# Eight row norms in a two-part transformer kernel: turning unscaled rows and multiplying the root in later

## What is computed

```python
def rms_norm(x, g):
    xf = x.astype(jnp.float32)
    y = xf * lax.rsqrt(jnp.mean(xf * xf, axis=-1, keepdims=True) + NORM_EPS)
    return (y * g.astype(jnp.float32)).astype(x.dtype)

h2 = rms_norm(x, g_ffn[l])
gt = causal_dwconv(h2 @ w_ffn_gate[l], ffn_conv_w[l])       # no convolution in the last two layers
x = x + (jax.nn.silu(gt) * (h2 @ w_ffn_up[l])) @ w_ffn_down[l]
```

## Time and profile before

| | us |
|---|---|
| median of 3 runs | 2024.78 (2019.59 to 2033.89) |
| the profiled execution | 2016.36 |
| its span, first to last instruction | 2014.3 |
| PE busy | 1810.7 (90%) |
| DVE / ACT / POOL busy | 1085.8 / 927.5 / 504.2 |
| weights and inputs read | 299.51 MB, 151 GB/s |

### The profile page before, as it was taken

The page is one execution under the profiler, slowest core; times in us unless marked ns, Lnnn a source line. Parts: engine busy times, 40 slices in busy tenths (PEclk is TensorE's granted clock), DMA queues, the critical chain, the costliest instruction groups (busy, mean ns, idle before and its releaser), DMA issues.

```text
span 2014.3 us, 31361 instructions
## 1 busy us (share of the span) xinstructions
PE 1810.7 (90%) x13399; PEld 1698.1 (84%) x13399; DVE 1085.8 (54%) x1671; ACT 927.5 (46%) x1198; POOL 504.2 (25%) x106
## 2 busy tenths in 40 slices
PE   3999999799989999997999887779999888779997
PEld 2999899699879999996998786559987887669986
DVE  3986666366449666664564457634452544434442
ACT  3456464344444565644444355443333554433432
POOL 0621000355416220003554000023443000023442
PEclk9999999899988999998999799689999899889999
DMA  4685445355544544553555533123555544234552
GB/s 152 182 220 170 147 131 204 105 171 186 209 131 151 186 158 142 165 185 100 193 169 206 154 126 105 63 84 121 173 179 197 159 136 125 84 105 141 173 201 81
DMA packets 248426, 305.73 MB, mean 152 GB/s; under 512 B 9706, under 2 KB 223934, under 8 KB 248287
## 3 DMA queue, kind: packets, MB, share of 16 engines
q1 hardware_dynamic: 233808, 288.08, 43.5%
q10 hardware_dynamic: 14479, 15.64, 3.6%
HBM read 299.51 MB, written 4.19 MB: 151 GB/s over the span
## 4 chain that ended last, share of the span: by engine, by line
PE 75%; DVE 13%; ACT 4%; DMA 3%; ACTq 3%; issue 2%; DVEq 0%
PE psum L439 23%; PE psum L440 23%; PE psum L441 23%; DVE wlo L415 6%; ACTq L370 2%; ACT whi L407 1%; DMA raw<-in_b_w_q 1%; ACTq L489 1%; DMA raw<-in_b_w_out 1%; ACT work L1793 1%; DVE work L2011 1%; PE psum L2208 1%; PE psum L655 1%; DVE stat L594 1%; DVE x L712 0%
## 5 line engine op out<-in xcount | busy, mean ns | idle before, releaser
L415 POOL TENSOR_TENSOR wlo<-raw,whi 128x2048 fp32r<-128x2048 f32 x100 | 503.1, 5031 | 1485.8 <-PE psum L441 1230.5
L439 PE MATMUL psum<-hT,whi 128*128 128x256 f32 x2544 | 730.3, 287 | 18.4 <-DVE wlo L415 16.6
L440 PE MATMUL psum<-hT,whi 128*128 128x256 f32 x2544 | 724.3, 285 | 0.0
L441 PE MATMUL psum<-hT,wlo 128*128 128x256 f32 x2544 | 723.9, 285 | 0.0
L407 ACT ACTIVATE whi<-raw 128x2048 fp32r<-128x2048 f32 (+2 forms) x277 | 523.8, 1896 | 317.2 <-PE psum L441 168.6
L415 DVE TENSOR_TENSOR wlo<-raw,whi 128x2048 fp32r<-128x2048 f32 x177 | 459.8, 2606 | 198.7 <-PE psum L441 178.4
L439 PEld LDWEIGHTS psum<-hT,whi 128*128 128x128 f32 x2544 | 493.1, 194 | 25.4 <-DVE wlo L415 19.6
L440 PEld LDWEIGHTS psum<-hT,whi 128*128 128x128 f32 x2544 | 493.1, 194 | 0.1
L441 PEld LDWEIGHTS psum<-hT,wlo 128*128 128x128 f32 x2544 | 492.5, 194 | 0.0
L439 PE MATMUL psum<-whi,hT 128*128 128x256 f32 (+3 forms) x544 | 171.8, 316 | 5.2 <-DVE hT L1497 4.4
L440 PE MATMUL psum<-wlo,hT 128*128 128x256 f32 (+3 forms) x544 | 171.2, 315 | 0.0
(11 more groups left out here) (286 smaller groups left out, 2237.1 us busy)
## 6 DMA issues: line engine op xcount, KB each, us to landing
raw<-in_w_in SPq DMA_DIRECT2D x78, 1024.0 KB, 5.4
raw<-in_ffn_w_up SPq DMA_DIRECT2D x44, 1024.0 KB, 5.1
raw<-in_w_ffn_gate SPq DMA_DIRECT2D x22, 1024.0 KB, 5.1
raw<-in_w_ffn_up SPq DMA_DIRECT2D x22, 1024.0 KB, 5.1
raw<-in_w_ffn_down SPq DMA_DIRECT2D x22, 1024.0 KB, 4.8
raw<-in_ffn_w_down SPq DMA_DIRECT2D x22, 1024.0 KB, 5.0
raw<-in_b_w_q SPq DMA_DIRECT2D x12, 1024.0 KB, 5.2
raw<-in_a_w_in SPq DMA_DIRECT2D x10, 1024.0 KB, 5.8
```

Of the source, the lines that this page charges most:

```text
L415: eng.tensor_tensor(part(wlo, n, LOW_SLOTS), part(raw, n, RAW_SLOTS), part(whi, n, HIGH_SLOTS).bitcast(F32), ALU.subtract).then_inc(stream ...
L439: nc.tensor.matmul(dst, left[0], right[0], start=first, stop=False)
L440: nc.tensor.matmul(dst, left[0], right[1], start=False, stop=False)
L441: return nc.tensor.matmul(dst, left[1], right[0], start=False, stop=last)
```

## The change

The norm stages are gone. The rows are turned as they are, without the root, and the root comes in later, by one of two ways.

- `add_rows_product` runs its last unit in the order of the two column halves, adds each quarter to `x` by itself, and turns the halves on PE at once into the four free banks (`turn_rows`); ACT and DVE split them with the gain alone (`high_rows`, `low_rows`) into `raw_T`. The squares are summed by quarters, the root is made, laid on a diagonal (`root_diag`), and after the next stage's first unit one matmul spreads it over all partitions (`spread_root`, `copy_root`, into `root_row`).
- The first unit of a stage is multiplied in the order in which the row pieces are made (`first_unit`). In the mixers and attentions the first 3 or 4 units use the unscaled rows and the root goes into their results; meanwhile DVE makes fully scaled rows (`whole_rows`, `whole_low`), which the later units use. The order of units in the attentions is changed for it.
- The feed-forward stages use the unscaled rows for all 22 units. DVE multiplies the gate by `root_row` out of PSUM (this replaces the ACT copy at L766), and multiplies the product of each pair by `root_row` once more, before the banks are released.
- Set-up loads the identity, one gain and the rows `x` first, the rest after unit 2 on SP's queue; the parameters are turned after the mixer's unit 1 and the distance tables made after unit 2. The rotary angles move from the start of the first mixer to between the two halves of its convolution.
- The last norm works in quarters and its gain is loaded a stage earlier. Tables of the attentions are loaded a few units later.

```diff
-            for first in (A_GL, A_KS, A_KW, A_VS, A_VW, A_Q, A_KC, A_VC, A_Q + S, A_Q + 2 * S):
+            for first in (A_GL, A_VS, A_VW, A_KS, A_KW, A_Q, A_KC, A_VC, A_Q + S, A_Q + 2 * S):
...
+            for part in (S, 0):
+                for n in range(len(DILATIONS)):
+                    u += column_units(a["kv_w_2"], 2 * S * n + part, 2 * S * n + part + S, "V")
...
+        def turn_rows(pe, base, ready):
+
+            for b in range(4):
+                if b % 2 == 0:
+                    pe.wait_ge(*ready[b // 2])
+                for j in range(4):
+                    k, t = 2 * b + j // 2, j % 2
+                    mm = nc.tensor.transpose(bank(base + b)[:, j * P:(j + 1) * P], x[:, t, k * P:(k + 1) * P], ident)
+                mm.then_inc(rows_turned.sem, 1)
...
+        def square_part(act, q):
+
+            h, t = q // 2, q % 2
+            squared = region(512 * q, 512)
+            ins = act.activation(squared, x[:, t, 512 * h:512 * (h + 1)], ACT.Square, accum_out=part_sum[:, q:q + 1])
+            if q == 3:
+                ins.then_inc(rows_squared.sem, 1)
...
+        def high_rows(act, base, dst, gain):
+
+            for b in range(4):
+                act.wait_ge(rows_turned.sem, rows_turned.at(b + 1))
+                for j in range(2):
+                    ins = act.activation(dst[0][:, 2 * b + j, :], bank(base + b)[:, j * S:(j + 1) * S], ACT.Copy,
+                                         scale=gain(2 * b + j))
+                ins.then_inc(rows_high.sem, 1)
...
+        def low_rows(dve, base, dst, gain):
+
+            for b in range(4):
+                dve.wait_ge(rows_high.sem, rows_high.at(b + 1))
+                for j in range(2):
+                    ins = dve.scalar_tensor_tensor(dst[1][:, 2 * b + j, :], bank(base + b)[:, j * S:(j + 1) * S],
+                                                   gain(2 * b + j), dst[0][:, 2 * b + j, :].bitcast(F32),
+                                                   ALU.mult, ALU.subtract)
+            ins.then_inc(rows_low.sem, 1)
...
+        def roots_of_rows(dve):
+
+            dve.wait_ge(rows_squared.sem, rows_squared.at(1))
+            v_link(dve.tensor_tensor(stat[:, 0:TT], part_sum[:, 0:TT], part_sum[:, TT:2 * TT], ALU.add))
+            inverse_root(dve, root, stat[:, 6:6 + TT], stat[:, 8:8 + TT], stat[:, 0:TT], 1.0 / D, 1)
+            for t in range(TT):
+                ins = dve.tensor_scalar(root_diag[:, t, :], ident, root[:, t:t + 1], None, ALU.mult)
+            ins.then_inc(root_made.sem, 1)
...
+        def spread_root(pe, base):
+
+            pe.wait_ge(root_made.sem, root_made.at(1))
+            nc.tensor.matmul(bank((base ^ 4) + 3)[:, 0:S], cst[:, C_ONE:C_ONE + P],
+                             root_diag.rearrange("p t s -> p (t s)"), start=True, stop=True).then_inc(root_turned.sem, 1)
...
+        def whole_rows(dve, base, kind, gain):
+
+            for k in range(KT):
+                ins = dve.scalar_tensor_tensor(whole_T[kind][:, k, :], bank(base + k // 2)[:, k % 2 * S:(k % 2 + 1) * S],
+                                               gain(k), root_row[:, :], ALU.mult, ALU.mult)
+                if k % 2:
+                    ins.then_inc(whole_ready.sem, 1)
...
+        def whole_high(act, dst, kind, b, turn=0):
+
+            act.wait_ge(whole_ready.sem, whole_ready.at(4 * turn + b + 1))
+            act.activation(dst[0][:, 2 * b:2 * b + 2, :], whole_T[kind][:, 2 * b:2 * b + 2, :], ACT.Copy) \
+               .then_inc(whole_taken.sem, 1)
+
+        def whole_low(dve, dst, kind, b, turn=0):
+
+            dve.wait_ge(whole_taken.sem, whole_taken.at(4 * turn + b + 1))
+            dve.tensor_tensor(dst[1][:, 2 * b:2 * b + 2, :], whole_T[kind][:, 2 * b:2 * b + 2, :],
+                              dst[0][:, 2 * b:2 * b + 2, :].bitcast(F32), ALU.subtract).then_inc(whole_split.sem, 1)
...
+        def first_unit(pe, w, src, tiles, by_columns):
+
+            wd = w[0].shape[2]
+            for b in range(4):
+                pe.wait_ge(rows_high.sem, rows_high.at(b + 1))
+                for j, dst in enumerate(tiles):
+                    for k in (2 * b, 2 * b + 1):
+                        first = b == j == 0 and k == 0
...
+            pe.wait_ge(rows_low.sem, rows_low.at(1))
...
+                    last = c == count - 1
+                    order = [(t, h) for h in range(2) for t in range(TT)] if last and kind else \
+                        [(t, h) for t in range(TT) for h in range(2)]
...
+                if kind:
+                    turn_rows(pe, base ^ 4, [(rows_added.sem, rows_added.at(2 * h + 2)) for h in range(2)])
...
+                make_high(act, n0 + count + 3)
...
+                    if q == 3 and kind:
+                        high_rows(act, base ^ 4, raw_T[kind], gain)
+                    act.wait_ge(rows_added.sem, rows_added.at(q + 1))
+                    square_part(act, q if kind else 2 * (q % 2) + q // 2)
+                if kind:
+                    square_root(act, stat[:, 6:6 + TT], stat[:, 8:8 + TT], 1)
...
+                    h, t = (q // 2, q % 2) if kind else (q % 2, q // 2)
+                    xs = x[:, t, 512 * h:512 * (h + 1)]
+                    dve.wait_ge(unit_used.sem, unit_used.at(count + q))
+                    dve.tensor_tensor(xs, xs, bank(base + 2 * t + h), ALU.add).then_inc(rows_added.sem, 1)
+                if kind:
+                    low_rows(dve, base ^ 4, raw_T[kind], gain)
+                    roots_of_rows(dve)
+                    make_lows(dve, n0 + count + 3)
...
-                    act.activation(gpad[:, c % 2, :, pad:], bank(2 * c % 4).rearrange("p (j s) -> p j s", j=2),
-                                   ACT.Copy).then_inc(scores_ready.sem, 1)
...
-                    v_link(dve.tensor_tensor(prod[:, c % 2], cacc[:, c % 2],
-                                             bank((2 * c + 1) % 4).rearrange("p (j s) -> p j s", j=2), ALU.mult))
+                    v_link(dve.tensor_tensor(prod[:, c % 2], cacc[:, c % 2], pair_of(2 * c + 1), ALU.mult))
+                    v_link(dve.tensor_tensor(prod[:, c % 2], prod[:, c % 2], spread(root_row[:, :], 1, 2), ALU.mult))
...
+                def gate(c):
+                    dve.wait_ge(bank_full.sem, bank_full.at(2 * c + 1))
+                    dst = cacc[:, c % 2] if conv is None else gpad[:, c % 2, :, pad:]
+                    v_link(dve.tensor_tensor(dst, pair_of(2 * c), spread(root_row[:, :], 1, 2), ALU.mult))
+                    if conv is None:
+                        nc.vector.nop().then_inc(gate_scaled.sem, 1)
+
...
+                def glu_gate(i):
+                    dve.wait_ge(bank_full.sem, bank_full.at(2 * i + 1))
+                    dve.tensor_tensor(sig[i], bank(0).rearrange("p (a s) -> p a s", a=2), spread(root_row[:, :], 1, 2),
+                                      ALU.mult).then_inc(dense_free[0].sem, 1)
+                    dve.wait_ge(dense_free[0].sem, dense_free[0].at(i + 1))
+                    nc.vector.nop().then_inc(gate_scaled.sem, 1)
...
+                    v_link(dve.tensor_tensor(dst, dst, spread(root_row[:, :], 1, 2), ALU.mult))
...
+                dve.wait_ge(root_spread.sem, root_spread.at(1))
+                glu_gate(0)
+                whole_rows(dve, turned, "mixer", norm_gain)
...
                 long_conv(0, 12, LONG)
                 v_wait(last[1])
                 nc.vector.nop().then_inc(conv_done.sem, 1)
+                if l == 0:
+                    rotary_angles(dve)
                 long_conv(1, 0, LONG)
```

More of the change, by code:

```diff
@@ L608, in close_roots @@
             root_ready.close(n)
-        def norm_stage(gain, scratch=0):
-            dst = hT
-            xn = region(scratch, TT, D)
+        raw_T = {}
+        whole_T = {}
+        for kind, rows_at, whole_at in (("mixer", 19088, 13312), ("ffn", 14400, 18496), ("blocks", 15456, 19552),
+                                        ("dilated", 17920, 22016)):
+            raw_T[kind] = [over(f"{kind}_rows{i}", at_work, rows_at + i * KT * S, [KT, S]) for i in range(2)]
+            whole_T[kind] = region(whole_at, KT, S)
@@ new lines, in _ @@
+                high_rows(act, base, raw_T[kind], gain)
+                for q in range(4):
+                    square_part(act, q)
+                square_root(act, stat[:, 6:6 + TT], stat[:, 8:8 + TT], 1)
+                make_high(act, 2)
+                end(act)
+            @block.tensor
+            def _(pe):
+                pe.wait_ge(ident_load.sem, ident_load.at(16))
+                pe.wait_ge(gain_load.sem, gain_load.at(16))
+                nc.tensor.transpose(bank(0)[:, 0:P], early, ident).then_inc(gains_turned.sem, 1)
+                turn_rows(pe, base, [(x_load[h].sem, x_load[h].at(16)) for h in range(2)])
+                end(pe)
@@ new lines, in distance_rows, with copy_parameters @@
+        def distance_rows(pe):
+            for n in range(4):
+                nc.tensor.matmul(bank((6, 7, 2, 3)[n])[0:QH, 0:SPAN], work[0:BUCKETS + 1, 24800:24800 + QH],
```

(23 more changed lines are left out.)

653 lines of the change are left out of this document (344 added, 309 removed).

## The result

The changed kernel takes 2054.8 us (median of 4 runs, 2050.53 to 2061.64) against 2022.9 us for the kernel before beside it: ratio 1.015, 95% interval 1.010 to 1.020. It is slower by 1 to 2%; the forecast was faster by 2.3%. The profiled span is 2048.7 us against 2014.3, so 34.4 us are to be found.

A forecast was written before the change was run, and what follows sets the result against it. PE, busy 90%, was taken as the bound, so only idle time could change. Boundaries, set-up, last norm and old waits gave -113.9 us, new waits 40 x 1.66: -47.5, so 2024.8 becomes 1977 us; range 1955 to 2005, wide 1935 to 2008.

The forecast's parts named there:

- The boundaries: Between stages: PE's idle 15.1 us becomes 2.3, a gain of 12.8 at each of four ahead of feed-forward stages.
- the last norm: At the kernel's end: quarters, the preloaded gain and overlapping halved stores gain 3 us.
- the set-up: Kernel start: reordered loads bring the first mixer's unit 4 to 45.5 us, from 68.5.
- The mechanism: Feed-forward pairs: second product delays DVE's low part, POOL goes first; low part or second product waits for the shared port.
- a wait of 1.66 us for the mean pair: Feed-forward stages: mean PE wait per pair over 40 pairs, in place of the old 18.3 us in all.
- a chance of 0.46: Feed-forward pair behind a stalled one: POOL starts before DVE's low part with this chance, giving a 2.4 us wait.
- Behind an unstalled pair: Feed-forward pairs: the next pair surely stalls, waiting 2.1 us in plain stages and 3.3 us with convolution.
- The convolved stages, forecast at 1.88, and the plain ones, at 1.45: Feed-forward stages with and without convolution: mean PE wait per pair, in us.
- rival two: Feed-forward stages: every pair falls into the long case, wait 3.4 us, kernel 22 us slower, 2047 us; chance 0.08.
- one wait of 8 to 10 us: First mixer, unit 14: PE waits behind ACT, held by DVE's late convolution and rotary angles; gain 14 us, not 23.
- forecast to lose 1.6 us: Second mixer: DVE's `whole_low` operations meet POOL's low parts, unit 4's rows come late, 1.6 us goes back.
- rival one: Feed-forward stages: second product avoids the port or low part always wins, wait stays 0.46 us; 1930 us; chance 0.22.

The follow-up runs named there:

- experiment 1: Kernel before plus one more 128x512 VectorE multiply, both operands in SBUF, between product and next low part in each feed-forward pair: 2127.0 us, ratio 1.051.
- experiment 4: Changed kernel with VectorE's low part for the next pair's up unit made before this pair's products: 1945.3 us, ratio 0.961 to the kernel before.
- experiment 8: Changed kernel with the root multiplied into the silu'd gate and the next pair's low part ahead of the product: 1919.1 us, ratio 0.950.
- experiment 9: Kernel with root in gate and low part first, plus the mixers' second gated product behind 6 instead of 12 convolution taps: 1896.9 us, ratio 0.937.
- experiment 6: Changed kernel with the up half's root multiplied into the silu'd gate before the up unit ends, not into the product: 1962.4 us, ratio 0.972.
- experiment 2: Kernel before plus an extra multiply between product and low part, with one operand read from PSUM: 2082.4 us, ratio 1.029.
- experiment 3: Kernel before plus an extra SBUF multiply of 0.7 us per pair, right behind VectorE's low part: 2038.7 us, ratio 1.0086.
- experiment 5: Changed kernel without the second multiply of each feed-forward pair, output not the reference's: 1927.7 us, ratio 0.953.

## Why the prediction was wrong

**The parts that were right.** The boundaries (13.2 us each against 12.8 forecast), the last norm, and the set-up (unit 4 of the first mixer starts at 45.4 us, forecast at 45.5). The mechanism too was right, and it was named: the second product puts VectorE's low part behind GpSimd's, which holds up either the low part or the second product itself. Experiments 1 and 4 show it from both sides.

**The step that failed first: how often.** The sum took a wait of 1.66 us for the mean pair, from a chance of 0.46 that GpSimd comes first behind a stalled pair. Measured is 2.48 us, and 37 of 40 pairs stall. Behind an unstalled pair the forecast held: all three such pairs stall, and all four first pairs of a stage do. Behind a stalled pair it did not: 30 of 33 stall (0.91). The trace splits these 33 by the clock.

- At the full clock (12 pairs) the up unit ends 5.7 to 5.9 us after the end of the last low part, and VectorE's next low part would ask 7.5 to 7.7 us after it. GpSimd starts 6.9 to 7.4 us after it in the ten pairs that stall, 7.9 and 8.8 in the two that do not. In the kernel before the same time was 7.1 to 9.3 us in 12 such pairs, six of them under 7.5: that spread gave the 0.46. Why GpSimd's data come at the early end of it here is not shown.
- With the low clock in the up unit (21 pairs) the unit ends 7.1 to 8.7 us after the last low part, VectorE asks later still, and 20 of the 21 stall. The forecast had no such pairs. How many of them would have stalled at the full clock is open.

In short, in the changed kernel one stall brings the next. The margin in the pair with GpSimd's start 1.5 us behind the unit's end was 0.5 us (VectorE's low part asked 1.0 us behind it), and 0.7 us were added. The convolved stages, forecast at 1.88, and the plain ones, at 1.45, came out alike (2.50 and 2.45).

**The step that was missing: the clock.** The up stages lost 82.6 us to waits on low parts (99.2 less 16.6). Even the right mean wait gives 40 x 2.48 - 18.3 = 80.9 us where 109.3 were lost. The rest is mainly TensorE at 1.2 GHz behind the waits, some 39 us against the floor of experiment 8. (In its windows the kernel before is busy 3 us each longer than that floor, 12.2 in all, with hardly a matmul at the low clock; I did not trace this, and it is why the two terms together give more than 109.3.) The forecast kept the full clock of the earlier trace rows while it put waits of 2 to 3 us into two pairs of three. Clock and waits together a pair lost (109.3 + 18.3) / 40 = 3.19 us, beyond the 2.85 from which rival two decides. That rival, every pair stalled, had the right end and nearly the right price (3.4), by waits alone, and a chance of 0.08; that its price fits is partly luck, since 0.7 us of it were clock.

**The mixers.** For the first mixer one wait of 8 to 10 us was forecast, at its unit 14 (counted from 0), behind ScalarE and the convolution with the rotary angles. The changed kernel has no wait there: unit 14 starts at 113.12 us, against 125.68 before, a gain of 12.6 where 14 were forecast, but for another reason. What I did not see is the sixth unit: it needs the bank that the second gated product reads, and that product stands behind 12 taps (`long_conv(0, 0, 12)`) on a VectorE which now starts late by the gate multiplies, the whole rows and the copies of the set-up. It waited 4.1 us in the first mixer, and the granted clock was at its low level from 55.0 to 68.7 us behind it; of the 23 us that unit 4 was ahead of the kernel before, unit 7 has 12.6 left (20.2 in experiment 9, without the wait). Another 2.7 us are waited at 140.7 (L1104), on ScalarE's squares for the channel means, with the low clock behind it again, and 8.2 us are left at the end. In the second mixer the sixth unit waited 4.4 us; that mixer was forecast to lose 1.6 us and lost 12.1. Experiment 9 takes away the wait, and 10 us with it in each mixer, and only then does the forecast wait at unit 14 appear, with 4.2 us at 109.84. The compressed attention's 8.2 us I have not tested: TensorE's idle time in it rose from 29.6 to 35.2 us in many small waits and one of 2.8.

**The balance.** From -47.5 the up stages take 61.2 more than forecast, the first mixer with the set-up 5.8, the second mixer 10.5, compressed and dilated 9.4; the boundaries and the last norm give 5.0 more. That is +34.4, what the spans show. That the first mixer with the set-up is off by 5.8 only is luck: its set-up was forecast well, its one wait was not where it was forecast, and another, with the clock, took about as much.

**What cures it.** Nothing in the change needs the second product where it stood. Multiplied into the gate, and with the low part ahead of the product, the same arithmetic (up to rounding) gives 1919 us, below the 1930 of rival one, the case with no added stall; with the two moves in the mixers 1889.5.

## What to carry to other kernels

An operation is priced by what stands behind it on its queue: the same 0.7 us cost 104 us ahead of the operation that TensorE waits for and 16 us behind it. Where two engines contend and one start follows from the other's last end, look at the margin in time between them and at what a turn that goes wrong does to the next turn's margin. And when a forecast puts repeated waits of 2 us and more on a TensorE that was hardly idle before, price the clock too: in the changed kernel, with waits of 2.3 to 4.1 us, a wait cost about 1.4 times its length. Shorter ones did not: the two plain up stages of experiment 6 have 17 us of waits, each of at most 1.8 us, at a clock of 1.00, and are 12 us longer than the floor.

## What the runs showed of the hardware

- While GpSimd's low part ran (4.6 us), VectorE's multiply with both operands in SBUF took 4.55 us, and the multiply of the same size with one operand in PSUM 0.69 us, started at the same point of the pair (experiments 1 and 2). The Trainium skill, page "SBUF — State Buffer", section "Who interferes with whom", says that a VectorE instruction with two inputs in SBUF contends with a GpSimd one that reads SBUF, for an exclusive lock, and that one with at most one input there, outside the two-port modes, does not; the traces agree on both, with the two times just given. It works the other way too: GpSimd's low part, recorded from 1395.61 us, ended 4.5 us after VectorE's low part had.
- The granted clock fell behind long waits in a busy stretch and not behind short ones. In eight of the traces (both kernels, experiments 1 to 6) TensorE waits 114 times for 1.75 us and more on a low part, and in 59 cases the granted clock is at its low level at some time in the 3 us behind the wait; of 92 shorter waits (0.4 to 1.75 us) none is followed so. The windows say the same: clock 1.00 in experiment 4, whose waits in the pairs are of at most 1.2 us, 0.91 to 0.96 in the changed kernel with 2.3 to 4.1 us. That the wait lowers the clock is read from this order of events; no run changes the one without the other.
